# ScalarE makes the high parts of all dense FFN units; pools of banks and the order of split places change

## What is computed

```
first block, twice:   x += w_out . (gated sum of three branches: mLSTM, sparse attention, differential attention)
                      x += w_down . (silu(xn . w_gate) * (xn . w_up))          xn = rms(x),  FF_DIM = 2816
second block, layer 1: x += retention(rms(x)) . ret_w_out   (4 heads, 512 values each, gated by silu)
                      x += w_down . (silu(xn . w_gate) * (xn . w_up))          D_FF = 3584
second block, layer 2: x += short_conv(rms(x)) . conv_w_out
                      x += sum over the top 2 of 8 experts of gate * swiglu_e(rms(x))
out = rms(x) * gain
```

## Time and profile before

| | us |
|---|---|
| three runs, median (lowest to highest) | 2657.95 (2655.5 to 2659.04) |
| the profiled execution | 2658.11 |
| its span in the profile | 2656.3 |
| PE busy | 2592.8 (98%) |
| DVE busy | 1803.0 (68%) |
| ACT busy | 1226.1 (46%) |
| POOL busy | 218.8 (8%) |

### The profile page before, as it was taken

One profiled execution on the slowest core, in us unless ns is written; L12 is line 12 of the kernel. 1 busy time (PEld: TensorE's weight loads), 2 busy tenths in 40 slices (PEclk: granted clock), 3 DMA queues, 4 the chain that ended last, 5 costly groups with the idle time before them and its releaser, 6 DMA issues.

```text
span 2656.3 us, 29239 instructions
## 1 busy us (share of the span) xinstructions
PE 2592.8 (98%) x11620; PEld 1989.4 (75%) x11620; DVE 1803.0 (68%) x1953; ACT 1226.1 (46%) x1423; POOL 218.8 (8%) x104
## 2 busy tenths in 40 slices
PE   8999999999999999999999998999999999999997
PEld 5455578865555888977788897878787888888886
DVE  3754555447445554745655567999999999999996
ACT  2233220023323102363100346777787877777775
POOL 0000023200000332000433100000000000000000
PEclk9999999999999999999999998999999999999999
DMA  6342455534334555545555455999999989999995
GB/s 214 129 154 100 158 192 189 170 110 137 127 113 170 193 190 173 184 157 175 175 190 190 143 176 181 375 325 381 320 379 325 377 324 376 325 355 347 354 345 188
DMA packets 273636, 610.13 MB, mean 230 GB/s; under 512 B 10476, under 2 KB 47522, under 8 KB 273338
## 3 DMA queue, kind: packets, MB, share of 16 engines
q1 hardware_dynamic: 273466, 607.67, 64.6%
HBM read 606.58 MB, written 1.05 MB: 229 GB/s over the span
## 4 chain that ended last, share of the span: by engine, by line
PE 90%; DVE 6%; ACT 3%; issue 1%; DMA 0%; SPq 0%; DVEq 0%; ACTq 0%
PE bank L467 87%; DVE split L1625 4%; PE bank L709 1%; PE bank L497 1%; ACT split L1195 1%; ACT parts L1195 0%; ACT xs L1195 0%; DVE tmp L1674 0%; DVE parts L1686 0%; ACT pbuf L1195 0%; DMA pbuf<-in_gain_rows 0%; DVE parts L1613 0%; ACT L1195 0%; ACT halves L1195 0%; DVE ybuf_tmp_high L1639 0%
## 5 line engine op out<-in xcount | busy, mean ns | idle before, releaser
L467 PE MATMUL bank<-split,parts 128*128 128x512 f32 (+1 forms) x6432 | 1463.3, 388 | 5.7 <-DVE split L1625 3.1
L467 PEld LDWEIGHTS bank<-split,parts 128*128 128x128 f32 x6432 | 1189.4, 188 | 247.3 <-issue 4.0
L1625 DVE TENSOR_TENSOR split<-ring,split 128x2048 fp32r<-128x2048 f32 x444 | 1020.4, 2344 | 81.9 <-POOL split L2251 60.9
L1195 ACT ACTIVATE split<-ring 128x2048 fp32r<-128x2048 f32 x344 | 659.6, 1921 | 187.0 <-PE bank L467 187.0
L467 PE MATMUL bank<-ring,xnT 128*128 128x512 f32 (+2 forms) x896 | 367.6, 567 | 0.0
L2251 POOL TENSOR_SCALAR split<-ring 128x2048 fp32r<-128x2048 f32 x100 | 218.6, 2187 | 1265.2 <-PE bank L467 1035.9
L467 PEld LDWEIGHTS bank<-ring,xnT 128*128 128x128 f32 x896 | 169.4, 190 | 180.0 <-issue 178.9
L1195 ACT ACTIVATE parts<-bank 128x512 fp32r<-128x512 f32 x128 | 68.8, 590 | 327.4 <-PE bank L709 327.4
L1639 DVE TENSOR_TENSOR halves<-ring,halves 128x1024 fp32r<-128x1024 f32 x96 | 116.4, 1224 | 84.1 <-ACT halves L1195 83.5
L1195 ACT ACTIVATE halves<-ring 128x1024 fp32r<-128x1024 f32 x96 | 101.3, 1059 | 153.9 <-PE bank L467 153.9
L1686 DVE TENSOR_TENSOR parts<-bank,parts 128x512 fp32r<-128x512 f32 x128 | 82.4, 686 | 124.9 <-ACT parts L1195 124.9
(11 more groups left out here) (260 smaller groups left out, 1861.1 us busy)
## 6 DMA issues: line engine op xcount, KB each, us to landing
ring<-in_moe_w_gate SPq DMA_DIRECT2D x112, 1024.0 KB, 8.0
ring<-in_moe_w_up SPq DMA_DIRECT2D x112, 1024.0 KB, 7.5
ring<-in_moe_w_down SPq DMA_DIRECT2D x112, 1024.0 KB, 7.5
ring<-in_w_gate_up SPq DMA_DIRECT2D x44, 1024.0 KB, 5.8
ring<-in_w_in SPq DMA_DIRECT2D x40, 1024.0 KB, 7.1
ring<-in_ret_w_in SPq DMA_DIRECT2D x24, 1024.0 KB, 5.1
ring<-in_w_down SPq DMA_DIRECT2D x22, 1024.0 KB, 5.1
ring<-in_w_in SPq DMA_DIRECT2D x20, 880.0 KB, 6.5
```

What stands on the lines that cost most here:

```text
L467: return nc.tensor.matmul(o, l, r, start=first, stop=final, **kw)
L1195: return nc.scalar.activation(out, in_, func, **kw)
L1625: V.tensor_tensor(split[:, split_place(m), 1, :], ring[:, n % RING, :], split[:, split_place(m), 0, :].bitcast(F32), ALU.subtract).then_in ...
```

## The change

GpSimd's stream is gone. ScalarE makes every high part of the dense FFNs, in an order by when each place is read. Split places follow 3, 0, 1, 2 instead of 3, 2, 0, 1 from the retention FFN on, and later halves are counted two places on. In the first block, two of the last four halves come ahead of the first FFN unit. `turn_merged(0)` takes LOW banks, the last branch and all of `turn_o` HIGH ones. DVE makes the retention FFN's second low part inside `to_ffn`. Three filler products stand ahead of the last `combine`.

```diff
--- before.py
+++ after.py
@@ -44,6 +44,7 @@
 SPLITS = 4
 HALVES = 4
 LAYER_HALVES = DEPTH * KT
+RET_HALVES = 8 * 2 + 8 * 4 + 2 * KT
 EARLY = 4
 PARAMS = 6
 GROUPS = D_FF // HALF
@@ -260,8 +261,7 @@
         for_dve = signal("bank_for_dve")
         act_freed = signal("act_emptied")
         dve_freed = signal("dve_emptied")
-        high_made = signal("weights_high")
-        high_act = signal("expert_weights_high")
+        high_act = signal("weights_high")
         half_high = signal("half_unit_high")
         half_low = signal("half_unit_low")
         low_made = signal("weights_low")
@@ -337,12 +337,17 @@
                 return place(n, (KT, 256))[:, :, j * P:(j + 1) * P]
             return ring[:, n % RING, j * (UNIT // 2):(j + 1) * (UNIT // 2)]
 
+        def half_place(h):
+
+
+            return (h if h < LAYER_HALVES + RET_HALVES else h + 2) % HALVES
+
         def place_half(h, by_column):
 
             if h < LAYER_HALVES:
                 whole = [late_halves[h % HALVES][:, i * (UNIT // 2):(i + 1) * (UNIT // 2)] for i in range(2)]
             else:
-                whole = [halves[:, h % HALVES, i, :] for i in range(2)]
+                whole = [halves[:, half_place(h), i, :] for i in range(2)]
             return [w.rearrange("p (k c) -> p k c", k=KT) for w in whole] if by_column else whole
 
         def group_units(i, groups):
@@ -370,18 +375,8 @@
 
             if m < DEPTH * layer_splits:
                 return m % SPLITS
-            return (3, 2, 0, 1)[(m - (DEPTH * layer_splits if m < dense_splits else dense_splits)) % SPLITS]
-
-        def high_of(m):
-
-
-
-            if m >= dense_splits:
-                return high_act, EARLY * DEPTH + m - dense_splits + 1
-            li = min(m // layer_splits, DEPTH)
-            if li < DEPTH and m % layer_splits < EARLY:
-                return high_act, EARLY * li + m % layer_splits + 1
-            return high_made, m + 1 - EARLY * min(li + 1, DEPTH)
+            return (3, 0, 1, 2)[(m - (DEPTH * layer_splits if m < dense_splits else dense_splits)) % SPLITS]
+
 
         block = ctx.enter_context(nc.Block())
 
@@ -417,8 +412,8 @@
             def new_stage():
 
 
-                half_free.extend(split_read[max(m for m in range(n_split[0]) if split_place(m) == h // 2)]
-                                 for h in range(HALVES))
+                half_free.extend(split_read[max(m for m in range(n_split[0]) if split_place(m) == half_place(h) // 2)]
+                                 for h in range(n_half[0], n_half[0] + HALVES))
 
             def take_half(j, by_column):
 
@@ -862,7 +857,7 @@
 
                 def turn_merged(h):
                     eng.wait_ge(mrg_dve.sem, pe.next(mrg_dve))
-                    turn_input(xs, (2 * h, 2 * h + 1), HIGH if h else ALL)
+                    turn_input(xs, (2 * h, 2 * h + 1), HIGH if h else LOW)
 
                 def branch(br):
                     eng.wait_ge(act_freed.sem, pe.point("branch", act_freed))
@@ -871,7 +866,7 @@
                         for tt in range(TT):
                             if br == 2 and (h, tt) == (1, 1):
                                 turn_merged(0)
-                            b = fill(ALL)
+                            b = fill(HIGH if br == 2 else ALL)
                             for k in range(4):
                                 ins = mm(bank[b][:, :], yT[:, br, k, tt * P:(tt + 1) * P],
                                          views[k // 2][:, k % 2, h * HALF:(h + 1) * HALF], k == 0, k == 3)
@@ -1037,11 +1032,11 @@
                 hand(ins, b, "act")
             point("ret_o")
 
-            def turn_o(h, pool=ALL):
+            def turn_o(h):
 
                 eng.wait_ge(rets_dve.sem, pe.next(rets_dve))
                 for fp in (2 * h, 2 * h + 1):
-                    transposes(lambda i: rv[:, i % 2, (2 * fp + i // 2) * P:(2 * fp + i // 2 + 1) * P], 4, "act", pool)
+                    transposes(lambda i: rv[:, i % 2, (2 * fp + i // 2) * P:(2 * fp + i // 2 + 1) * P], 4, "act", HIGH)
                     point("input")
                     give_low(last_bank[0])
 
@@ -1053,7 +1048,7 @@
 
             def o_ready(k):
                 if k == 4:
-                    turn_o(RH - 1, HIGH)
+                    turn_o(RH - 1)
                     point("o turned")
                 if k % 2 == 0:
                     eng.wait_ge(x_low.sem, o_at + k // 2)
@@ -1135,6 +1130,7 @@
 
             def combine(big, ends=False):
 
+                filler(3 if ends else 0)
                 eng.wait_ge(act_freed.sem, pe.point("y", act_freed))
                 eng.wait_ge(act_freed.sem, pe.point("put", act_freed))
                 outs = [(fill((4, 5, 6, 7)), tt, h) for tt in range(TT) for h in range(2)]
@@ -1299,17 +1295,33 @@
                     copy(hidden(0, late)[:, 0:n // P, tt * P:(tt + 1) * P],
                          view=lambda b: b[:, 0:n].rearrange("p (f t) -> p f t", t=P))
 
-            def ffn_act(groups, gain):
+            def ffn_act(groups, gain, first):
+
+
+                ups = [group_units(i, groups)[0] for i in range(len(groups))]
+                downs = [n // 256 for _, n in groups]
+                total = units_of(groups)
+
+                def highs_to(count):
+                    count = first + min(count, total)
+                    expert_high(max(0, count - nth_split[0]), first)
+
                 highs(gain, pairs=(0, 1))
                 square(BY_HALF)
                 highs(gain, pairs=(2, 3))
+                highs_to(SPLITS)
                 roots(xsum[:, 2, :], xsum[:, 1, :])
                 eng.wait_ge(rstd_dve.sem, act.next(rstd_dve))
-                for i in range(len(groups) + 1):
+                read = 0
+                for i in range(len(groups)):
                     if i:
-                        hidden_high(groups[i - 1][1], i == len(groups))
-                    if i < len(groups):
-                        gated(groups[i][1], normed=False)
+                        hidden_high(groups[i - 1][1], False)
+                    highs_to(read + ups[i] + SPLITS)
+                    gated(groups[i][1], normed=False)
+                    read += 2 * ups[i] + (downs[i - 1] if i else 0)
+                    highs_to(read - (1 if i + 1 == len(groups) else 0) + SPLITS)
+                hidden_high(groups[-1][1], True)
+                assert nth_split[0] == first + total
 
             def experts_act():
                 for e in range(NE):
@@ -1445,11 +1457,11 @@
                     for kp in (2 * h, 2 * h + 1):
                         copy(merged_parts[0][:, 2 * kp:2 * kp + 2, :].rearrange("p f t -> p (f t)"))
                     half_highs(1)
-                for _ in range(EARLY):
-                    half_highs(1)
+                for n in (2, 1, 1):
+                    half_highs(n)
                     expert_high(1, layer_splits * li)
-                nth_split[0] += layer_splits - EARLY
-                ffn_act(groups1, G_FFN + 8 * li)
+                expert_high(EARLY - 3, layer_splits * li)
+                ffn_act(groups1, G_FFN + 8 * li, layer_splits * li)
 
             def setup():
 
@@ -1503,8 +1515,13 @@
             half_highs(4)
             o_highs()
             half_highs(8)
-            ffn_act(groups2, G_FFN0)
-            nth_split[0] += units_of(groups2)
+            first = layer_splits * DEPTH
+            expert_high(1, first)
+            for h in range(LAYER_HALVES + RET_HALVES - HALVES, LAYER_HALVES + RET_HALVES - 2):
+                sig, value = half_read[h]
+                eng.wait_ge(sig.sem, value)
+            expert_high(1, first)
+            ffn_act(groups2, G_FFN0, first)
 
 
             half_highs(2)
@@ -1620,8 +1637,7 @@
                 for _ in range(units):
                     n, m = unit_of_split[nth_split[0]], nth_split[0]
                     nth_split[0] += 1
-                    sig, value = high_of(m)
-                    eng.wait_ge(sig.sem, value)
+                    eng.wait_ge(high_act.sem, m + 1)
                     V.tensor_tensor(split[:, split_place(m), 1, :], ring[:, n % RING, :],
                                     split[:, split_place(m), 0, :].bitcast(F32),
                                     ALU.subtract).then_inc(low_made.sem, low_made.tick())
@@ -1661,9 +1677,10 @@
                     ins.then_inc(dve_freed.sem, dve_freed.tick())
                 eng.wait_ge(dve_freed.sem, dve.latest(dve_freed))
 
-            def to_ffn(gain):
+            def to_ffn(gain, units=0):
                 for h in range(2):
                     add_to_x(BY_HALF[2 * h:2 * h + 2])
+                    weights_low(units if h else 0)
                     lows(gain, pairs=(2 * h, 2 * h + 1))
 
             def hidden_product(n, normed=True):
@@ -2051,9 +2068,10 @@
                 turned_low(2)
                 turned_low(3)
                 half_lows(1)
-                for _ in range(4):
-                    half_lows(1)
+                for n in (2, 1, 1):
```

(33 more changed lines are left out.)

## The result

| | us |
|---|---|
| before, six runs, median (lowest to highest) | 2657.59 (2655.5 to 2659.93) |
| changed kernel, six runs | 2667.35 (2664.84 to 2668.13) |
| ratio, 95% interval | 1.0033 (1.0021 to 1.0045) |
| profiled execution of the changed kernel, its span | 2668.13, 2666.4 |

The change makes the kernel slower: by 9.8 us between the two medians, and by 0.33% (8.8 us) by the ratio over all runs. The forecast was 2661 and "within 0.2%". The median lies 0.35 us above the range's upper end of 2667 (the ratio, put on the 2657.95 us of the forecast, gives 2666.7, just inside), on the side to which I had given 0.25.

A forecast was written before the change was run, and what follows sets the result against it. TensorE, busy 98% of the span, was taken to bound the kernel. The terms -2.6 + 0.2 + 8.7 + 3.5 - 4.0 - 0.9 - 1.8 = +3.1 us on 2658.11 gave 2661 us, range 2652 to 2667.

The forecast's parts named there:

- the chunk for head 2: Retention output: turn_o(0) waits for bank 4, then this chunk waits for its turned bank; starts 6.0 us later.
- The second stall: Retention output: turn_o(1) waits for ScalarE's copies in the same way, delaying the next chunk; +4.6 us.
- the clock: Retention output: the granted clock falls behind each of the two new gaps; 2 x 1.75 = +3.5 us.
- the output product: Retention output: loses its 3.53 us wait but still needs bank 0 emptied; -1.9 us.
- The start of the layers' FFNs: Layers 0 and 1: bank wait goes in layer 0, late half unit comes earlier in both; -2.6 us together.
- the router: Router: its first turned bank is now an earlier one, so PE's 0.88 us wait goes; -0.9 us.
- the retention FFN's start: Retention FFN: second unit's low part is made earlier, so PE goes on without the 3.13 us wait; -4.0 us.
- The rest: Places outside the main stages: router wait gone, -0.9 us, and filler products before the last combination, -1.8 us.
- The narrow groups: Narrow last FFN group of the two layers: later hidden copies eat DVE's reserve; 0.1 us per layer, +0.2.
- (b): Rival: the retention turns don't stall because the banks come out otherwise; 2647 us, chance 0.10.
- (d): Rival: dense groups come to wait for ScalarE, 1 us in each of 19 groups; 2680 us, chance 0.04.
- (c): Rival: clock falls in both gaps, end's fillers don't hold it, retention FFN keeps half its gain; 2665 us, chance 0.23.

The follow-up runs named there:

- Kernel 2: Changed kernel with only the eight-bank pool's counter moved on, by 3 ahead of the three retention chunks and 5 behind: 2652.97 us, ratio 0.9982.
- Kernel 3: Changed kernel with only the eight-bank pool's counter moved on, by 4 ahead of and 4 behind the retention and convolution input turns: 2661.07 us, ratio 1.0012.
- kernel 7: Changed kernel with turn_o on ALL except its last turn, the counter moved on for the retention input, and two ScalarE orders changed: 2643.96 us, ratio 0.9945.
- kernel 1: Changed kernel with turn_o drawing from ALL again, except its last turn on HIGH: 2645.13 us, ratio 0.9956.
- Kernel 5: Changed kernel with the bank pools of the kernel before and without the filler products at the end: 2657.46 us, ratio 0.9994.
- kernel 4: Changed kernel with only the eight-bank pool's counter moved on, at both the retention output and the two inputs: 2646.76 us, ratio 0.9957.
- kernel 6: Kernel before, GpSimd work kept, with only the pools of turn_merged(0), the last branch and turn_o changed: 2680.44 us, ratio 1.0074.

## Why the prediction was right and where it failed

**The terms that were priced.** The wait at 1194.45 begins the chain as I had it: bank 4 is emptied behind a half, a table load and two copies, PE turns then, and the chunk for head 2 starts 6.1 us later than before (predicted 6.0). The second stall cost 4.3 (4.6), the clock 1.9 and 1.5 us in the two chunks (3.5 together), and the output product gained 2.2 (1.9). Kernel 2 takes all of it away: from the changed kernel's profile to its own, 13.5 us at this place. That is 1.9 more than the changed kernel had lost here (8.2 + 3.4 = 11.6), as the 3.53 us ahead of the output product stay away too. The start of the layers' FFNs, the router and the retention FFN's start came out within 0.4 us each. There PE passes from the first unit on without the 3.13 us of the earlier trace rows, the clock stays up, and it waits 0.77 for the third low part, the one behind the root.

The two-column addition of the earlier trace rows had taken 1.84 us beside GpSimd. In DVE's timeline of the changed kernel it is

```profile
1282.03 0.15 DVE L1594 TENSOR_TENSOR xsum<-xhalf 128x2 f32<-128x2 f32 x1
```

and the mean subtraction went from 2344 to 2285 ns. The Trainium skill, SBUF — State Buffer (on the shared port pair), has GpSimd and such DVE instructions exclude each other; both numbers agree. The prediction gave this no part in the time. But the low part that PE waited for in the earlier trace rows was itself made beside GpSimd, and took 3.71 us where such a subtraction takes 2.29:

```profile
1268.64 3.71 DVE L1625 TENSOR_TENSOR split<-ring,split 128x2048 fp32r<-128x2048 f32 x1
```

By that row some 1.4 of the 3.13 us were this contention. The new order makes that low part earlier in any case (at 1278.00, in 2.29 us), so no run tells what of the 4.0 us the absence of GpSimd would have given alone.

**The step that failed.** "The rest" and the sum took every place outside the listed ones to be free of new bank waits. I had counted the fills of the retention output and of the layers' output products, and looked no further at the counter of ALL behind them. It changed for every later stage, and `input_split` is a place where a fill of LOW follows at once on fills of ALL. (The convolution's output product is another; its wait of 0.94 us before and 0.78 after changed little.) The filler's 3.22 us stall costs 2.1 us at the retention input and 1.7 by the clock behind it, and 1.5 at the convolution's, where it had been 1.66 us long before: 5.3 of the missing 7.3 us. That entry of the list before (2.5 us for DVE xparts, twice, at most 1.7) stood in the trace, and the list of single places in the prediction left it out; followed up, it would have shown the mechanism. Kernel 3 removes 6.3 us by moving that counter alone, and leaves the rest of PE's waits.

**Sizes.** The narrow groups cost 0.25 us each instead of 0.1, as the hidden copies' delay did eat more than the reserve. In kernel 7, with the copy behind them, all of it came back, which shows the cause.

**The clock at the experts' start.** The 48 matmuls at 1641.67 took 12.80 us, their first 4 us at a granted clock of 0.57, where the same 48 before took 11.22 at 1.00 (timeline, then window columns as above):

```profile
1631.64 11.22 PE L467 MATMUL bank<-split,parts 128*128 128x512 f32 x48 [2.08 <-DVE parts L1613]
1631.50:1635.50 4.00, 3.86 (x17) 3.17 (x18) 4.00 (x2) 0.71 (x1) 0.00 (x0) 1.00 0.21 30
```

The gap ahead of them is 2.08 us in both. I had no term for it. With another 0.4 us in the 32 small matmuls ahead of the gap (6.36 us against 5.90) it is the 2.0 of the table. No run gives the cause, but the ten profiles rule two out. The 48 matmuls take 11.2 us in the kernel before and in kernels 1 and 2, and 12.7 to 12.8 in all others. Kernel 5 has the banks of the kernel before and is slow here, and kernels 1 and 2 have the work of the changed kernel and are not, so neither the banks alone nor ScalarE's work alone decides it. It stays open.

**Rivals.** (b) and (d) are excluded: the turns stalled as counted, and the dense groups kept their pace. (c) is right by its time and wrong by its mechanism: the end's fillers held the clock, and the retention FFN kept its whole gain. What put the time past the forecast was a mechanism none of them had.

**What the change is worth.** Its parts have opposite signs. A counter can give back 20.6 us (kernel 4); the remainder, 2658.55 - 2646.76 = 11.8 us, is what that kernel gains on the one before. Not all of the 20.6 is loss by the change: 1.9 us at the retention output and 0.8 at the convolution's input were bank waits of the kernel before. From the table I get as much: 2.0 + 0.7 - 0.5 + 4.0 + 1.3 + 1.5, with the 1.9 and the 0.8, make 11.7. (Kernel 4's profile is only 10.2 us shorter than the one before, as it has the low clock at the experts' start.) The output product's part, the router's and most of layer 0's come from the pools as well; kernel 5, which has the work without any pool changed, gave 1.5 us or nothing by its time, and 4.8 at the places of its profile that the work touches.

## What to carry to other kernels

A shared counter of banks makes every use downstream part of an edit: when one use leaves a pool, count the fills of every pool to the end of the program, before and after, and look at each fill of another pool that follows closely on banks handed to a slow reader. Look for such a wait in the kernel before as well, however short it is there. Filler work that is to cover a wait must not take a bank, or anything else, from what it waits for. To tell a rotation from a load, move only the counter: it costs no work, and here its effects added up place by place.

## What I had not expected of the hardware

- A gap of PE of 3.53 us at the same instruction left the granted clock at 1.00 in the kernel before and was followed by 7 us at a mean of 0.62 in kernel 5; the gap of 2.08 us at the experts' start was followed by 1.00 before and 0.57 after the change. The Trainium skill, TensorE: Matmul & The Clock Gate (The HAM clock gate), has the clock fall after idling; these pairs show that for gaps of 2 to 4 us the gap's length alone doesn't decide. Each fall behind a gap cost some 1.5 to 3 us, and the one in kernel 6 without a gap 3.8, so two kernels' profiles can differ by some microseconds for this alone.
- The first 128 products of the program took 29.53 us before and 29.56 after, but 27.87 in PE's timeline of kernel 1, which has the same instructions there:

```profile
15.88 27.87 PE L462 MATMUL bank<-xnT,ring 128*128 128x256 f32 x128 [1.02 <-ACT xnT L1191]
```

What differs is how long the start runs slowly. In kernels 1 and 2 these products start 0.22 us apart from the first on; in the other eight profiles the first 7 to 10 of them start 0.43 us apart, twice as far, and the rest 0.22. That is why kernels 1, 2 and 7 were compared stage by stage and not by their spans. I have not found what decides it.
